# A hybrid decoder layer on one Trainium2 core: expert up-projection weights loaded in 2 MB pieces, two neighbouring rows to a partition

## What is computed

```python
def _moe(x, w_router, b_router, w_up, b_up, w_down, b_down):
    logits = (x @ w_router + b_router).astype(f32)
    top_v, top_i = lax.top_k(logits, TOP_K)            # 4 of 32
    top_w = jax.nn.softmax(top_v, axis=-1)
    ...
    def expert_step(acc, ep):
        w1, b1, w2, b2, g = ep                         # w1: 1024 x 2048, w2: 1024 x 1024
        hdn = x @ w1 + b1
        gt = jnp.minimum(hdn[:, :D_FF], SWIGLU_LIMIT)
        up = jnp.clip(hdn[:, D_FF:], -SWIGLU_LIMIT, SWIGLU_LIMIT)
        act = (up + 1.0) * gt * jax.nn.sigmoid(SWIGLU_ALPHA * gt)
        return acc + g[:, None] * (act @ w2 + b2), None
```

## Time and profile before

| | us |
|---|---|
| three runs | 1344.64, 1346.15, 1350.28 |
| median | 1346.15 |
| the profiled execution | 1345.19 |
| its span, first to last instruction | 1343.4 |
| TensorE busy in it | 1249.5 (93%) |
| VectorE, ScalarE, GpSimd busy | 371.6, 182.1, 98.8 |
| granted TensorE clock, mean | 0.962 of full speed |

### The profile page before, as it was taken

The page is one execution under the profiler, slowest core; times in us unless marked ns, Lnnn a source line. Parts: engine busy times, 40 slices in busy tenths (PEclk is TensorE's granted clock), DMA queues, the critical chain, the costliest instruction groups (busy, mean ns, idle before and its releaser), DMA issues.

```text
span 1343.4 us, 15541 instructions
## 1 busy us (share of the span) xinstructions
PE 1249.5 (93%) x5839; PEld 595.0 (44%) x5839; DVE 371.6 (28%) x700; ACT 182.1 (14%) x338; POOL 98.8 (7%) x214
## 2 busy tenths in 40 slices
PE   3997888899999999999999999999999999999875
PEld 3754665443434343434344343434344343434354
DVE  6899724112121111111221111111211211121233
ACT  2113322101010110101110101101110101100022
POOL 4665300000000000000000000000000000000000
PEclk8996998999999999999999999999999999998888
DMA  9322123597999999999999999999999999998400
GB/s 312 124 93 100 41 99 126 213 395 319 422 382 412 418 405 423 384 423 407 422 406 423 403 411 420 404 423 405 422 402 422 396 415 411 405 382 366 184 1 33
DMA packets 72238, 438.45 MB, mean 326 GB/s; under 512 B 13616, under 2 KB 16816, under 8 KB 21472
## 3 DMA queue, kind: packets, MB, share of 16 engines
q1 hardware_dynamic: 71632, 437.60, 80.2%
q10 hardware_dynamic: 576, 0.45, 0.1%
HBM read 436.65 MB, written 2.41 MB: 327 GB/s over the span
## 4 chain that ended last, share of the span: by engine, by line
PE 88%; DVE 6%; issue 2%; ACT 2%; DMA 0%; ACTq 0%; DVEq 0%; SPq 0%
PE ps L908 38%; PE ps L925 18%; PE ps L894 10%; PE ps L864 5%; PE ps L797 2%; PE ps L1037 2%; PE ps L511 2%; PE ps L916 2%; PE ps L591 1%; PE ps L867 1%; PE ps L556 1%; PE ps L980 1%; PE ps L934 1%; PE ps L599 1%; PE ps L760 1%
## 5 line engine op out<-in xcount | busy, mean ns | idle before, releaser
L908 PE MATMUL ps<-ring_up,region 128*64 128x512 f32 x2112 | 463.5, 597 | 2.6 <-issue 1.4
L908 PEld LDWEIGHTS ps<-ring_up,region 128*64 128x64 f32 x2112 | 163.8, 138 | 284.3 <-issue 282.4
L925 PE MATMUL ps<-ring_dn,region 128*64 128x512 f32 x1056 | 246.9, 622 | 12.4 <-issue 11.0
L1684 DVE TENSOR_SCALAR region<-ps 128x512 f32<-128x512 f32 x33 | 22.8, 692 | 716.4 <-PE ps L908 716.4
L925 PEld LDWEIGHTS ps<-ring_dn,region 128*64 128x64 f32 x1056 | 82.6, 142 | 163.6 <-issue 161.5
L894 PE MATMUL ps<-region,n_tok 128*128 128x128 f32 (+1 forms) x768 | 136.1, 307 | 0.0
L894 PEld LDWEIGHTS ps<-region,n_tok 128*128 128x128 f32 (+1 forms) x768 | 104.2, 187 | 41.2 <-issue 12.2
L1226 ACT ACTIVATE region<-region 128x512 f32<-128x512 f32 x33 | 20.8, 630 | 501.3 <-DVE region L1684 501.3
L478 POOL COPY region<-kst 128x64 f32 (+1 forms) x33 | 7.8, 238 | 990.8 <-PE ps L908 990.8
L1238 ACT ACTIVATE region<-ps 64x512 f32<-64x512 f32 x66 | 39.1, 592 | 269.9 <-PE ps L925 269.5
L864 PE MATMUL ps<-region 128*128 128x512 f32 (+1 forms) x136 | 65.9, 606 | 2.6 <-issue 1.3
(11 more groups left out here) (354 smaller groups left out, 886.7 us busy)
## 6 DMA issues: line engine op xcount, KB each, us to landing
ring_up<-in_w_up_dram SPq DMA_DIRECT2D x264, 1024.0 KB, 12.0
ring_dn<-in_w_down_dram SPq DMA_DIRECT2D x132, 1024.0 KB, 7.9
ring_up<-in_w_in_dram SPq DMA_DIRECT2D x4, 1280.0 KB, 10.0
ring_dn<-in_w_out_dram SPq DMA_DIRECT2D x1, 4096.0 KB, 25.0
ring_up<-in_w_ple_gate_dram SPq DMA_DIRECT2D x4, 1024.0 KB, 7.1
x_tok<-in_x_prompt_dram SPq DMA_DIRECT2D x2, 512.0 KB
ring_up<-in_w_glu_dram SPq DMA_DIRECT2D x1, 1024.0 KB, 15.0
region<-in_w_ple_proj_dram SPq DMA_DIRECT2D x1, 1024.0 KB
```

Source lines behind the costliest of these rows:

```text
L908: m = mm(ps[64 * (q % 2):64 * (q % 2) + 64, q // 2, :], xe[:, k, slots] if k < UP else one_hot, w, start=(k == 0), stop=(k == UP))
L925: m = mm(ps[64 * half:64 * half + 64, O_B, :], act_t[:, f % 4, 64 * (f // 4):64 * (f // 4) + 64], ring_dn[:, f, 512 * half:512 * half + 51 ...
L1684: V.tensor_scalar(g_lim, bank(0), LIMIT, None, ALU.min).then_inc(Z["g_rdy"], 1)
```

## The change

`w_up` is loaded in four transfers of 2 MB per expert, each with two neighbouring rows in a partition (16 KB in a run). Partition p of transfer s holds rows 256s+2p and 256s+2p+1, so block k of the tokens must hold the features 256(k//2) + 2j + k%2: the gather reads every second column of `n_tok`, and the gain is needed in that order too, so it is loaded once more as four rows of 256 and transposed with two further transposes into eight new columns of `vecs`. A ring slot now is 2 MB, and `up_free` counts four to an expert.

```diff
-V_MIX, ..., V_GLU, V_N = 0, 8, 16, 24, 32, 36, 40
+V_MIX, ..., V_GLU, V_ROW, V_N = 0, 8, 16, 24, 32, 36, 40, 48
-UP, DN = 8, 4
+UP, DN = 4, 4
@@ SyncE
-            up_w = A["w_up"][0].rearrange("e (k p) n -> e k p n", p=P)
+            up_w = A["w_up"][0].rearrange("e (s p k) n -> e s p k n", p=P, k=2)
                 for k in range(UP):
-                    if first and k == 5:
+                    if first and k == 2:
                         embedding_loads()
                     if first:
-                        sp.wait_ge(*((Z["q_ps"], 6) if k < 5 else (Z["glu_ps"], KM) if k == 5 else (Z["s5_free"], 1)))
+                        sp.wait_ge(*((Z["q_ps"], 6) if k < 2 else (Z["glu_ps"], KM) if k == 2 else (Z["s5_free"], 1)))
                     else:
                         sp.wait_ge(Z["up_free"], t * UP + (k + 1 - UP))
-                    sp.dma_start(ring_up[:, k], up_w[bass.ds(e, 1), k].rearrange("e p n -> (e p) n")
+                    sp.dma_start(ring_up[:, 2 * k:2 * k + 2], up_w[bass.ds(e, 1), k].rearrange("e p k n -> (e p) k n")
                                  ).then_inc(up_in[k], 16)
...
             for k in range(4):
-                sp.wait_ge(Z["up_free"], (n + (NE - 1)) * UP + (k + 1))
+                sp.wait_ge(Z["up_free"], (n + (NE - 1)) * UP + (k // 2 + 1))
@@ TensorE
-            pe.wait_ge(ld_vec, 16 * 7)
-            tr(bank(7, V_N), rows[0:V_N, 0:P], ident[0:V_N, 0:V_N]).then_inc(Z["vec_ps"], 1)
+            pe.wait_ge(ld_vec, 16 * 8)
+            tr(bank(7, V_ROW), rows[0:V_ROW, 0:P], ident[0:V_ROW, 0:V_ROW])
+            in_pairs = rows[64:68, 0:2 * P].rearrange("s (n k) -> s k n", k=2)
+            for k in range(2):
+                m = tr(ps[:, 7, V_ROW:V_ROW + 8].rearrange("p (s k) -> p k s", k=2)[:, k], in_pairs[:, k], ident[64:68, 64:68])
+            m.then_inc(Z["vec_ps"], 1)
+            n_by_row = n_tok[:].rearrange("p c (s n k) -> p c s k n", s=4, k=2)
@@ gather (gather_visit likewise)
-                        m = mm(ps[:, X_B[k // 4], ...], n_tok[0:nt, c, k * P:(k + 1) * P],
+                        m = mm(ps[:, X_B[k // 4], ...], n_by_row[0:nt, c, k // 2, k % 2],
@@ up
-                for k in range(UP + 1):
-                    if k < UP:
-                        pe.wait_ge(up_in[k], 16 * t + 16)
-                    else:
+                for k in range(KD + 1):
+                    if k == KD:
                         pe.wait_ge(Z["hot_rdy"], t + 2)
+                    elif k % 2 == 0:
+                        pe.wait_ge(up_in[k // 2], 16 * t + 16)
                     for q in range(4):
...
-                    m.then_inc(Z["up_free"] if k < UP else Z["hid_ps"], 1)
+                    if k == KD:
+                        m.then_inc(Z["hid_ps"], 1)
+                    elif k % 2 == 1:
+                        m.then_inc(Z["up_free"], 1)
@@ ScalarE
+            act.dma_start(rows[64:68, 0:2 * P], A["norm_ffn"][0].rearrange("(s n) -> s n", s=4)).then_inc(ld_vec, 16)
@@ VectorE, gathered (gathered_visit likewise)
-                                    col(vecs[:, V_FFN + 4 * h:V_FFN + 4 * h + 4], 2 * C), ALU.mult
+                                    col(vecs[:, V_ROW + 4 * h:V_ROW + 4 * h + 4], 2 * C), ALU.mult
```

More of the change, by code:

```diff
@@ L64 @@
 K_N = K_OF + 4
-V_MIX, V_FFN, V_PLE, V_OUT, V_D, V_GLU, V_N = 0, 8, 16, 24, 32, 36, 40
+V_MIX, V_FFN, V_PLE, V_OUT, V_D, V_GLU, V_ROW, V_N = 0, 8, 16, 24, 32, 36, 40, 48
 AT_KVTOK, AT_SCORES, AT_VALUES, AT_TURN = 6, (6, 9), (8, 12), (11, 15)
@@ L121, in hybrid_layer @@
         ps = ctx.enter_context(nc.psum_tensor("ps", [P, 8, 512], F32))
-        ring_up = sb("ring_up", [P, UP, 2 * FF])
+        ring_up = sb("ring_up", [P, 2 * UP, 2 * FF])
         ring_dn = sb("ring_dn", [P, 2 * DN, D])
@@ L893, in gather @@
                     for c, (t0, nt) in enumerate(CHUNKS):
-                        m = mm(ps[:, X_B[k // 4], (k % 4) * P:(k % 4 + 1) * P], n_tok[0:nt, c, k * P:(k + 1) * P],
+                        m = mm(ps[:, X_B[k // 4], (k % 4) * P:(k % 4 + 1) * P], n_by_row[0:nt, c, k // 2, k % 2],
                                sel[0:nt, c].rearrange("p a s -> p (a s)"), start=(c == 0), stop=(c == 2))
@@ L899, in up @@
             def up(t, slots):
-                for k in range(UP + 1):
-                    if k < UP:
-                        pe.wait_ge(up_in[k], 16 * t + 16)
-                    else:
+                for k in range(KD + 1):
+                    if k == KD:
                         pe.wait_ge(Z["hot_rdy"], t + 2)
+                    elif k % 2 == 0:
+                        pe.wait_ge(up_in[k // 2], 16 * t + 16)
                     for q in range(4):
-                        w = (ring_up[:, k] if k < UP else b_up)[:, q * 512:(q + 1) * 512]
-                        m = mm(ps[64 * (q % 2):64 * (q % 2) + 64, q // 2, :], xe[:, k, slots] if k < UP else one_hot, w,
-                               start=(k == 0), stop=(k == UP))
-                    m.then_inc(Z["up_free"] if k < UP else Z["hid_ps"], 1)
+                        w = (ring_up[:, k] if k < KD else b_up)[:, q * 512:(q + 1) * 512]
+                        m = mm(ps[64 * (q % 2):64 * (q % 2) + 64, q // 2, :], xe[:, k, slots] if k < KD else one_hot, w,
+                               start=(k == 0), stop=(k == KD))
+                    if k == KD:
+                        m.then_inc(Z["hid_ps"], 1)
+                    elif k % 2 == 1:
+                        m.then_inc(Z["up_free"], 1)
             def turn_activations(t):
@@ L979, in gather_visit @@
                     for c, (t0, nt) in enumerate(CHUNKS):
-                        m = mm(ps[:, 2, k * C:(k + 1) * C], n_tok[0:nt, c, k * P:(k + 1) * P], sel[0:nt, c, 0],
+                        m = mm(ps[:, 2, k * C:(k + 1) * C], n_by_row[0:nt, c, k // 2, k % 2], sel[0:nt, c, 0],
                                start=(c == 0), stop=(c == 2))
@@ L1730, in gathered_visit @@
                 V.tensor_tensor(xe[:, :, 0:C], ps[:, 2].rearrange("p (k s) -> p k s", k=KD),
-                                col(vecs[:, V_FFN:V_FFN + KD], C), ALU.mult).then_inc(Z["xe_rdy"], 1)
+                                col(vecs[:, V_ROW:V_ROW + KD], C), ALU.mult).then_inc(Z["xe_rdy"], 1)
             def visit(v, e):
```

## The result

The changed kernel takes 1349.97 us in the median of 20 runs, the one before 1345.51 us in as many: a ratio of 1.0034, with a 95% interval from 1.0027 to 1.0042. That is 4.5 us more. It is 1.5 us over the forecast of 1348.5 us and inside the half per cent that the prediction called "same", but slower beyond the noise of this many runs. One of the 20 executions of the changed kernel took 2549.05 us, at full granted clock; it is left out of the ratio, and nothing on record says why it was so long.

A forecast was written before the change was run, and what follows sets the result against it. The prediction took TensorE to bound the kernel: 1345.2 us (profiled execution) + 3.3 us for the gather, all else 0, gave 1348.5 us. Its own range was 1344 to 1352 us; for 8 in 10, 1342 to 1366.

The forecast's parts named there:

- The bound: Expert loop: TensorE bounds at 30.42 us per expert; loads have some 0.9 us per expert to spare.
- The larger pieces at 0: Loads of w_up: half as many transfers, first slot freed 1.72 us later, at least 8.7 us left; effect 0.
- The gather: Its 816 stationary loads at every second column: between 0 and 20 ns each, taken as 4 ns, +3.3 us.
- Start and end at 0: Extra gain load, two transposes, wider copy at the start, later embedding gate load at the end: all covered, 0.
- The sum: Whole kernel: 1348.5 us, +2.4 us over the median; "same" meant within half a per cent, 1339.4 to 1352.9; chance 0.61.
- A: Gather: each strided load costs 20 ns, as in the batch of transposes; 1361.5 us, slower; chance 0.16.
- B: Gather: the strided read adds its whole 69 ns to each load; 1401 us; chance 0.07.
- G: Gather: the strided load is free; 1345.2 us, on the forecast's side and 0.35 of its chance.
- C: Expert loads become the bound, through slower 16 KB packets or the later first piece; 1363 us at 406 GB/s; chance 0.05.
- D: TensorE's clock: falls to half vanish, 1338 us, chance 0.04, or four more come, 1355.3 us, chance 0.04.
- E: Loads of w_up: transfers are cut into the same packets as before; same sum, no chance given.
- F: Ahead of the down-projection: fewer transfers let activations through sooner, the 11.0 us idle goes; 1337.5 us; chance 0.03.

The follow-up runs named there:

- big_loads_only: The changed kernel with its gather reading neighbouring columns again, so that it computes something else; 1346.05 us, ratio 1.0013 to the kernel before.
- turned_once: The changed kernel with columns put in order once by VectorE, the gather reading neighbouring columns and no second gain copy; 1345.93 us, ratio 0.9997 to the kernel before.
- half_up_2mb: The changed kernel with two of the up-projection's four column parts left out, all loads kept; 1282.57 us, ratio 0.9519 to the kernel before.

## Why the prediction held, point by point

**The bound.** Right. TensorE bounded, and its waits are the same to the tenth of a microsecond after the change.

**The larger pieces at 0.** Right, by `big_loads_only` and `turned_once`, and for the reason given: the lead, 9.1 us against the 8.7 worked out. At 427 against 422 GB/s the rate, left open in the prediction, moved the good way.

**The gather.** The mechanism was right, the size was off: predicted 4 ns a load, 3.3 us in all, measured 0.31/48 = 6.5 ns, which over 816 loads is 5.3 us. The fifth of the way to 20 ns was a choice without a row. Measured it is a third. The argument behind it, that a gather's load comes 173 ns after the last and so has room for 114 ns of strided reading, was the wrong comparison, because the 173 are a mean over spacings of 112 and of more than 200 ns. The room was not there in the wide spacings either: they too grew by 6 to 7 ns. Had I taken the tight ones, 112 against the 117 to 120 that the matmuls of the strided transposes keep in the same trace, 5 to 8 ns would have come out. The statement that duration is not the cost held for the transposes (69 ns longer, 20 ns later) but not for the gather, whose loads became 7 ns longer and 6.5 ns later.

**Start and end at 0.** Right to about a microsecond, but not at 0: the longer start delays the input projection by some 0.75 us in the profiles, and what of it reaches the end is smaller than the scatter. The prediction had priced only ScalarE's wait and TensorE's idle time, and had not followed the start up to the input projection. Which part of the longer start does it, the load or the transposes, stays open.

**The sum.** 1348.5 against 1349.97 us, 1.5 us short. The gather alone was 2.0 us short; the 0.3 us from the profiled execution (1345.19) to the median of 20 (1345.51) adds to that, and some 0.8 us went the other way, within the runs' scatter. So near a hit of the total is partly luck.

**The rivals.** A (20 ns everywhere) and B (69 ns) fell, as the load's own spacing of 112 ns hides all but 6 ns. G (the stride is free) fell by the gather's 0.31 us. C did not occur, and `half_up_2mb` shows that where loads bound the large pieces help. D stayed small: the mean clock is 0.960 against 0.962, with three of the nine stretches from 300 to 1200 us at 0.98 instead of four. Its price on the fast side, 1338 us, had left out the gather's 3.3 us; with them it is 1341.7 us, which is not "faster". E fell: the trace holds 53237 packets instead of 72238, those of 16 KB at 611 ns in the median against 309 for 8 KB. F fell: the 11.0 us stayed.

## What to carry to other kernels

A better transfer is worth nothing while another engine bounds, so the price of matching the data to it must be paid off that engine: here VectorE did the reordering once, for 0.01 us per row block, where TensorE paid 0.31 us in each gather. Look at the spacing of instructions inside a block, not at its mean: the two levels in the gather, 112 and over 200 ns, showed where 50 us lay, and the smaller one is what a stride has to be held against. And when a bound is removed, a ring's lead hides the next one for a while.

## What the runs showed of the hardware

- A float32 stationary load of 128 columns keeps matmuls 112, 118, 174, 234 and 239 ns apart at column strides of 1, 2, 3, 4 and 8. With the clock at its lower level it is 213, 213, 213, 233 and 235 to 240 ns.
- At stride 3 and 4 the mean granted clock was 0.898 and 0.881 instead of 0.962; it fell in the gather and stayed low behind it.
- Changing between 128-row and 8-row stationary operands cost TensorE its overlap: 48 matmuls take 8.51 us with every third pair on 8 rows and 5.62 us with all on 128. Whether 8-row operands among themselves would overlap no run here shows.
- With a queue that is always full, 422 GB/s are moved in runs of 8 KB per partition, and 427 GB/s with `w_up`, two thirds of the bytes, in runs of 16 KB.
